# Block 2 of a two-block sequence model: the decay's ScalarE work under one table set, and a new place for its sum, for the bias, and for the keys' SiLU, scores and squares

## What is computed

```python
def hybrid_layer(x, ...):
    h = rmsnorm(x, norm_w)
    proj = h @ w_in                       # 1024 x 3752, split into the parts below
    y_mla  = mla_mixer(m_cq, m_ckv, m_kr, ...) * silu(m_gate)
    y_gdn  = gdn_mixer(g_q, g_k, g_v, g_z, g_b, g_a, ...)
    y_moba = moba_mixer(c_q, c_k, c_v, t5_table) * silu(c_gate)
    return x + concatenate([y_mla, y_gdn, y_moba]) @ w_out

def gdn_mixer(q, k, v, z, b, a, conv_w, A_log, dt_bias, norm_w):
    q, k, v = silu(causal_conv([q, k, v], conv_w))        # four taps
    q = l2norm(q) * 128 ** -0.5;  k = l2norm(k)           # needs sums of squares
    beta = sigmoid(b)
    g = -exp(A_log) * softplus(a + dt_bias)
    gc = cumsum(g)                                        # "the decay's sum"
    decay = exp(gc[t] - gc[j]) where t >= j
    L = beta * (k k^T) * decay, strictly lower            # "the keys' scores"
    ...                                                   # (I + L)^-1, then the chunked delta rule
```

## Time and profile before

| | |
|---|---|
| median of 3 runs | 1376.73 us |
| profiled execution | span 1369.2 us, first to last instruction (no other time of it is recorded) |
| TensorE busy | 1345.0 us (98%) |
| VectorE, ScalarE, GpSimd busy | 1040.0 (76%), 750.9 (55%), 46.3 us (3%) |
| granted TensorE clock, mean of the span | 0.996 of full speed |
| the two layers of block 2 | from about 1020 us and from about 1196 us to the end |

### The profile page before, as it was taken

One profiled execution on the slowest core, in us unless ns is written; L12 is line 12 of the kernel. 1 busy time (PEld: TensorE's weight loads), 2 busy tenths in 40 slices (PEclk: granted clock), 3 DMA queues, 4 the chain that ended last, 5 costly groups with the idle time before them and its releaser, 6 DMA issues. The chain is left out here.

```text
span 1369.2 us, 26498 instructions
## 1 busy us (share of the span) xinstructions
PE 1345.0 (98%) x10828; PEld 1265.4 (92%) x10828; DVE 1040.0 (76%) x1781; ACT 750.9 (55%) x1157; POOL 46.3 (3%) x48
## 2 busy tenths in 40 slices
PE   8999999999999999999999999999999999999998
PEld 8899999998999989899999999999989899888996
DVE  6999898677766666999897767766778746777565
ACT  6544656556444455544557545544558546576363
POOL 0000000000000000000000000000000110001100
PEclk9999999999999999999999999999999999999999
DMA  8565444564665465645364555555553324353231
GB/s 289 177 207 178 131 154 160 180 215 155 197 202 185 139 230 163 215 155 185 97 204 159 187 187 172 198 185 191 178 186 124 120 64 137 100 174 109 78 102 69
DMA packets 108992, 223.77 MB, mean 163 GB/s; under 512 B 6180, under 2 KB 17700, under 8 KB 108872
## 3 DMA queue, kind: packets, MB, share of 16 engines
q1 hardware_dynamic: 106736, 219.12, 48.2%
q10 hardware_dynamic: 2136, 2.96, 0.7%
HBM read 221.01 MB, written 1.06 MB: 162 GB/s over the span
## 5 line engine op out<-in xcount | busy, mean ns | idle before, releaser
L1755 DVE TENSOR_TENSOR wlo<-ring,whi 128x1024 fp32r<-128x1024 f32 (+3 forms) x430 | 498.1, 1180 | 182.7 <-ACT whi L1173 152.7
L1173 ACT ACTIVATE whi<-ring 128x1024 fp32r<-128x1024 f32 (+3 forms) x430 | 433.2, 1026 | 361.8 <-PE bank L499 228.7
L499 PE MATMUL bank<-hhi,whi 128*128 128x256 f32 x2016 | 278.8, 280 | 6.0 <-ACT sgb L1431 3.9
L508 PE MATMUL bank<-hhi,wlo 128*128 128x256 f32 x2016 | 280.3, 281 | 0.0
L499 PE MATMUL bank<-hlo,whi 128*128 128x256 f32 x2016 | 275.3, 278 | 0.0
L499 PEld LDWEIGHTS bank<-hhi,whi 128*128 128x128 f32 x2016 | 253.1, 189 | 9.5 <-ACT sgb L1431 4.3
L508 PEld LDWEIGHTS bank<-hhi,wlo 128*128 128x128 f32 x2016 | 252.6, 189 | 3.7 <-issue 2.6
L499 PEld LDWEIGHTS bank<-hlo,whi 128*128 128x128 f32 x2016 | 251.6, 189 | 0.0
L469 PE MATMUL bank<-w 64*64 64x64 f32 (+5 forms) x1376 | 101.7, 249 | 1.5 <-DMA w<-in_flip 0.9
L1935 DVE SCALAR_TENSOR_TENSOR w<-w,par 128x256 f32<-128x256 f32 x240 | 98.0, 478 | 0.0
L521 PE MATMUL bank<-whi,hhi 128*128 128x512 f32 (+2 forms) x256 | 96.6, 379 | 0.0
(11 more groups left out here) (309 smaller groups left out, 1535.5 us busy)
## 6 DMA issues: line engine op xcount, KB each, us to landing
ring<-in_w_in SPq DMA_DIRECT2D x100, 1024.0 KB, 5.1
ring<-in_w_ffn_down SPq DMA_DIRECT2D x22, 1024.0 KB, 5.1
ring<-in_w_ffn_gate SPq DMA_DIRECT2D x20, 1024.0 KB, 5.1
ring<-in_w_ffn_up SPq DMA_DIRECT2D x20, 1024.0 KB, 5.1
ring<-in_w_merge SPq DMA_DIRECT2D x8, 1024.0 KB, 5.1
ring<-in_w_out SPq DMA_DIRECT2D x8, 1024.0 KB, 5.0
ring<-in_w_oc SPq DMA_DIRECT2D x4, 1024.0 KB, 5.3
ring<-in_w_od SPq DMA_DIRECT2D x4, 1024.0 KB, 5.2
```

Of the source, the lines that this page charges most:

```text
L499: done = e.matmul(o, wh[:, k, cols(u)], s_[:, k0 + k, :], stop=False, skip_group_check=True, start=opens and k == 0 and s_ is sh and u % 2 ...
L508: done = e.matmul(o, wl[:, k, cols(u)], sh[:, k0 + k, :], start=False, stop=closes, skip_group_check=True)
L1173: e.activation(part_of(whi, j), part_raw(j), ACT.Copy).then_inc(*up("hi.a"))
L1755: e.tensor_tensor(part_of(wlo, j), part_raw(j), part_of(whi, j), ALU.subtract).then_inc(*up("lo.v"))
```

## The change

The plan's numbers move: the bias by one place, decay 2 and decay 3 by one, taps 0 by one, delta 0 by one, delta 1 and 2 by two. The task taps now stands behind others and decay in the table, so that at a shared place it runs after them. The six warm-up matmuls ahead of the decay's sum are gone. ScalarE loads a table set that holds both Exp and Ln by name ahead of the decay's first function.

```diff
 TWO_PLAN = {
-        "bias": [5, 5, 5, 6],
-        "taps": [12, 20, 34],
+        "bias": [6, 6, 6, 7],
         "others": [28, 34, 41, 41, 53],
-        "decay": [10, 10, 11, 12],
-        "delta": [17, 18, 20, 20, 30, 30, 36, ...],
+        "decay": [10, 10, 12, 13],
+        "taps": [13, 20, 34],
+        "delta": [18, 20, 22, 22, 30, 30, 36, ...],
...
                 bk = ps.take(e, "s", "gsum", l)
-                awake(bk, 6)
                 e.wait_ge(*at("gv", l))
...
             def decay_a(l):
                 yield 0
+                e.preload_act_table_set("natural_log_exp_and_others")
                 e.activation(ea, prm("alog", l), ACT.Exp).then_inc(*up("decay.a"))
```

More of the change, by code:

```diff
@@ L92 @@
 TWO_PLAN = {
-        "bias": [5, 5, 5, 6],
-        "taps": [12, 20, 34],
+        "bias": [6, 6, 6, 7],
         "others": [28, 34, 41, 41, 53],
-        "decay": [10, 10, 11, 12],
-        "delta": [17, 18, 20, 20, 30, 30, 36, 37, 39, 41, 43, 46, 46, 48, 48, 50, 51, 52, 53, 54, 55, 62, 65, 66, 66],
+        "decay": [10, 10, 12, 13],
+        "taps": [13, 20, 34],
+        "delta": [18, 20, 22, 22, 30, 30, 36, 37, 39, 41, 43, 46, 46, 48, 48, 50, 51, 52, 53, 54, 55, 62, 65, 66, 66],
         "latent": [26, 29, 30, 34, 36, 37, 39, 43, 46, 53, 54, 65, 66],
@@ L169 @@
     tensor_tensor = tensor_scalar = scalar_tensor_tensor = tensor_copy = same
-    tensor_reduce = reciprocal = max = match_replace = same
+    tensor_reduce = reciprocal = max = match_replace = preload_act_table_set = same
 SEMS = ("hi.a", "lo.v", "first.p", "second.p", "init.v",
```

## The result

The changed kernel took 1391.2 us (median of 4 runs, 1387.8 to 1392.5) against 1376.5 for the kernel before: a ratio of 1.0104, 95% interval 1.0089 to 1.0118, so slower by 14.3 us (12 to 16). The prediction had 1388.5, in a range of 1384.3 to 1392.1.

The account below looks back on a forecast made before the run. TensorE was taken as the bound; waits at the keys' squares, less gains, summed to +8.8 us and the clock's fall added 3.0: 1376.7 + 11.8 = 1388.5 us, range 1384.3 to 1392.1.

Parts of the forecast that it names:

- The chain: ScalarE and VectorE work ahead of the keys' squares, ending at A + 23.0; TensorE waits from A + 15.7, 7.3 us per layer.
- A: Point on TensorE's timeline that times are counted from: where the warm-up starts before the change, the start of part 6 after.
- The clock: Behind TensorE's 7.3 us wait at the sum of the keys' squares: clock falls to 1.2 GHz, +3.0 us in all.
- I take 1.5 per layer, +3.0 in all: Time lost at half clock behind the long wait, taken from the program's start, where 1.5 us were lost.
- the upper bound, 3.0 per layer: Clock loss behind the long wait if the slow stretch lasts twice as long as at the program's start.
- the rival that the clock holds: The wait at the sum of the keys' squares comes but the clock doesn't fall: 1385.5 us, chance 0.17.
- what lies around it: The median of the runs is 7.5 us above the profiled execution's span of 1369.2; the same difference was applied there.
- The waits for g and the flip matrix: TensorE's waits for the decay's g (1.8 us in two) and the bias's flip matrix (0.9 us in one) go.
- the gains of the removed warm-up, g and the bias are sure: TensorE saves 2.74 us in the second layer, 2.1 in the first, and 0.9 from the bias in the first.
- Longer table loads: Rival: the load left in ScalarE's chain is longer by 1.4 us per layer; about 1391.3 us, chance 0.05.

Follow-up runs that it names:

- squares_early: Changed kernel with ScalarE squaring the keys at place 18, ahead of the queries' SiLU; ratio 0.9988 to the kernel before, 1369.6 against 1371.3 us.
- squares_between: Changed kernel with ScalarE squaring the keys between the two halves of the queries' SiLU; ratio 1.0013 to the kernel before, 1373.4 against 1371.3 us.
- wait_filled: Changed kernel with 28 matmuls of ones on TensorE ahead of the sum of the keys' squares; ratio 1.0054 to the kernel before, 1379.4 against 1371.3 us.
- changed_wide: Changed kernel with both sums of squares streaming 64 columns of ones instead of one; ratio 1.0098 to the kernel before.
- sums_wide: squares_early with both sums of squares streaming 64 columns of ones instead of one; ratio 0.9971 to the kernel before, 1372.8 against 1375.6 us.
- only_no_warm: Kernel before without the six warm-up matmuls; ratio 1.0014 to the kernel before, 1378.4 against 1375.6 us.
- only_bias: Kernel before with the bias one place later and nothing else; ratio 0.9999 to the kernel before.
- before_wide: Kernel before with both sums of squares streaming 64 columns and nothing else; ratio 1.0003 to the kernel before.

## Why the prediction was right

*Direction and mechanism.* Right: squares_early takes the wait away by moving the squares alone, and squares_between sets it to 2.2 us. The list of the program already showed it; the rows gave the size.

*The chain.* Counted from A: the keys' SiLU was to end at A + 11.4 and ended at A + 11.2 (1229.15); the scores were to start at A + 11.6 and started at A + 11.5, without a wait; the queries' last taps at A + 21.75, measured 21.2; the sum of squares at A + 23.0, measured 22.5. TensorE's arrival was right to 0.1 us, since its own pace can be read off. The wait was 6.7 and 6.8 us for 7.3. The 0.5 us missing are mostly that the queries' first taps began 0.4 us sooner (A + 14.0 for 14.4) and that L2376 twice took 0.2 us less than counted.

*The clock.* That it falls was right, the size wrong: the term "I take 1.5 per layer, +3.0 in all" was mis-sized. TensorE worked at half clock for 6.4 and 7.9 us, which is 3.2 + 3.9 = 7.1 us lost, and wait_filled got back 6.9. The row it was taken from the earlier trace rows is a start from rest, where the slow stretch was 2.9 us long; behind a wait of 6.8 us it was over twice that. Even the upper bound, 3.0 per layer, was too low: the two layers lost 3.2 and 3.9. changed_wide shows that the one-column passes aren't the reason; what is stays open.

*Why the total came out near.* The waits were 1.2 us shorter than counted and the clock cost 4.1 more: +2.9, and 1388.5 + 2.9 = 1391.4, where 1391.2 was measured. That the total lies inside the range is in part luck: with the clock's measured cost and the waits as counted it would have been 1392.6, above the upper end of 1392.1.

*Two readings that were wrong.* The prediction says of the granted clock that the record shows 1.00 everywhere but at the very end. Block 1 shows otherwise, in the kernel before (waits of TensorE, then stretches with columns as in the earlier trace rows):

```profile
PE bank L499 <- ACT sgb L1431: 3.9, 2, 2.0
150.00:200.00 50.00, 48.02 (x378) 47.02 (x378) 43.91 (x82) 31.80 (x45) 0.00 (x0) 0.97 0.40 127
650.00:700.00 50.00, 48.04 (x379) 47.04 (x378) 43.91 (x84) 31.76 (x44) 0.00 (x0) 0.97 0.40 127
```

The clock fell at 167.8 and at 669.6, 0.5 and 1.5 us after the end of a wait of 2.0 us, and stayed down for 3.4 us each time, with 1.7 us lost. So a wait far shorter than 7.3 us could bring it down, which speaks against the rival that the clock holds, and a price near the 1.5 us that was taken lay in the record; that a long wait costs twice as much did not. The other reading is that the median is 7.5 us above the profile's span for "what lies around it". In every run whose span is recorded the time is 1.8 us above the span; the rest is that the profiled execution was faster than the others. The difference forecast doesn't hang on it.

*The gains.* The waits for g and the flip matrix went as said. But "the gains of the removed warm-up, g and the bias are sure", 5.7 us, was too much: with the long wait away, squares_early kept 1.7 and sums_wide 4.0. What is missing lies in the clock, which the prediction took for steady outside the long wait, and in small new waits: two falls cost squares_early 3.4 us, and sums_wide, with none in its profile, has 2.7 us of waits instead.

*Longer table loads.* After the change the load ahead of the keys' SiLU starts at 1226.70, 0.02 us after the last Exp ends (1226.05 and 0.63 us), takes 1.28 us, and the SiLU starts at 1228.00, again 0.02 us later. This rival can be dropped. The Trainium skill, in "ScalarE: Activation LUTs", section "What ACT_TABLE_LOAD costs", adds a drain of about 1.38 us to each load; this trace doesn't agree, on either side of the load.

## What to carry to other kernels

When steps share an in-order engine, moving one that a busier engine waits for behind one that waits for a third engine joins two chains that had nothing to do with each other; look at what stands ahead of the producer, not at when its own inputs are ready. Where TensorE is the bound, a wait costs its length and then the clock: fill it, or keep it short. And before a change of many parts is judged, run its parts: here one line of it, the named table set, was worth 3.7 us alone (2.1 to 5.2), and the whole lost 14.

## What the runs showed of the hardware that wasn't expected

The granted clock fell without a wait to speak of. In squares_early it fell right behind 16 passes of a 128 x 128 weight load and one streamed column, in the one layer with no wait ahead of them, in the other with one of 0.66 us; with 64 columns and the same 1.8 us it didn't, in the one profile that there is of it. After waits of 2.0 and 2.67 us (only_no_warm) it fell in both layers, after waits of 1.2 us now and then (only_bias, before_wide). After a wait of 6.8 us it stayed down for 10.2 us, behind the others for 3.4 us.

The same program doesn't always fall at the same place. Block 1 is the same in all these kernels. The profile of the kernel before has two falls in block 1, that of the changed kernel one, that of only_no_warm none, and in each of the three TensorE's longest wait there for ScalarE's L1431 (L1430 in the other two) is 2.0 us. So in this kernel a difference of 0.1% between two orders can be the clock alone. The mean granted clock of the runs, beside the time, tells whether it is; where the falls lie only the profile tells, and it is one execution.
